# Cross attention's query and output products: from split weights to plain fp32, one token half after the other

## What is computed

```python
x = x + merged @ w_out                             # "wo2": the mixer's output product
h = rmsnorm(x, norm_xa_g)
q = (h @ w_q).reshape(B, S, 4, 128)                # "xq"
k, v = split(rmsnorm(mem, norm_mem_g) @ w_kv)      # made earlier in the kernel
p = softmax(einsum("bshd,bmhd->bhsm", q, k) * 128 ** -0.5)
x = x + einsum("bhsm,bmhd->bshd", p, v) @ w_o      # "xo"
h = rmsnorm(x, norm_ffn_g)
qq = (h @ w_q_peer).reshape(T, 8, 2, 128)          # "pq": the expert queries
s = einsum("thpd,hpnd->thpn", qq, subkeys)         # head scores, two lists of 128 a head
# top 16 of each list, top 16 of their 256 sums: 16 experts e with softmax weights g
a = gelu(einsum("td,thkd->thk", h, w_down[e]))
x = x + einsum("thk,thkd->td", g * a, w_up[e])
return rmsnorm(x, final_g)
```

## Time and profile before

| | us |
|---|---|
| median of 3 runs | 1304.25 |
| lowest and highest | 1302.63, 1304.44 |
| profiled execution, its span | 1302.2 |
| PE busy | 1188.0 (91%) |
| DVE busy | 920.6 (71%) |
| ACT busy | 545.5 (42%) |
| POOL busy | 285.0 (22%) |
| bytes moved by the DMA engines | 396.67 MB, of them 268.45 MB by gathers |

### The profile page before, as it was taken

The page is one execution under the profiler, slowest core; times in us unless marked ns, Lnnn a source line. Parts: engine busy times, 40 slices in busy tenths (PEclk is TensorE's granted clock), DMA queues, the critical chain, the costliest instruction groups (busy, mean ns, idle before and its releaser), DMA issues.

```text
span 1302.2 us, 16734 instructions
## 1 busy us (share of the span) xinstructions
PE 1188.0 (91%) x5950; PEld 845.7 (65%) x5950; DVE 920.6 (71%) x1836; ACT 545.5 (42%) x983; POOL 285.0 (22%) x261
## 2 busy tenths in 40 slices
PE   9999999999999999999999889999777877777776
PEld 9998999888888999998865545545322332332322
DVE  6885858777854865567797777776767777777655
ACT  5833655566533547536643333322322222222312
POOL 0000000000000000000145455443643444544420
PEclk9999999999999999999999999999999999989999
DMA  7544456455655654456799999999999999999996
GB/s 287 194 166 148 167 200 213 169 178 183 225 195 194 213 176 160 164 196 230 318 408 402 420 419 420 419 420 419 420 420 418 421 419 422 419 422 419 420 420 262
DMA packets 55925, 396.67 MB, mean 305 GB/s; under 512 B 6320, under 2 KB 6320, under 8 KB 8624
## 3 DMA queue, kind: packets, MB, share of 16 engines
q0 software_dynamic: 36864, 268.45, 49.9%
q1 hardware_dynamic: 17136, 119.16, 25.6%
q10 hardware_dynamic: 1856, 8.13, 1.8%
HBM read 394.67 MB, written 1.05 MB: 304 GB/s over the span
## 4 chain that ended last, share of the span: by engine, by line
PE 56%; DMA 31%; DVE 6%; issue 3%; ACT 3%; POOL 2%; DVEq 0%; POOLq 0%; ACTq 0%
DMA R<-experts,IDX 31%; PE ps L606 19%; PE ps L707 10%; PE ps L1190 8%; PE ps L926 4%; PE ps L654 3%; PE ps L928 2%; POOL R L2778 2%; PE ps L618 2%; DVE R L2564 2%; PE ps L674 1%; PE ps L1041 1%; PE ps L1095 1%; ACT DIAG L1645 1%; PE ps L1068 1%
## 5 line engine op out<-in xcount | busy, mean ns | idle before, releaser
L1190 PE MATMUL ps<-R,DIAG 128*128 128x512 f32 x1020 | 484.6, 623 | 102.7 <-ACT DIAG L1645 97.5
L1190 PEld LDWEIGHTS ps<-R,DIAG 128*128 128x128 f32 x1020 | 191.5, 197 | 371.3 <-issue 206.9
L2564 DVE CUSTOM_DVE_ANT_0 R<-R,XN 128x1024 f32<-128x1024 f32 x256 | 313.4, 1227 | 143.5 <-DMA R<-experts,IDX 137.8
L2778 POOL DMA_INDIRECT R<-experts,IDX x256 | 283.7, 1108 | 535.4 <-PE ps L1190 278.4
L1774 DVE TENSOR_TENSOR w_lo<-raw,w_hi 128x1024 fp32r<-128x1024 f32 x204 | 241.7, 1220 | 89.3 <-ACT w_hi L1243 84.9
L1243 ACT ACTIVATE w_hi<-raw 128x1024 fp32r<-128x1024 f32 x203 | 204.7, 1051 | 78.0 <-DMA raw<-weights 78.0
L1633 ACT ACTIVATE act_d<-dots,rst 128x2 f32<-128x2 f32 (+1 forms) x130 | 38.5, 296 | 329.4 <-DVE dots L2564 329.2
L1645 ACT ACTIVATE DIAG<-con,coef 128x128 f32<-128x128 f32 x255 | 88.6, 394 | 121.3 <-DVE coef L2573 118.1
L606 PE MATMUL ps<-both_C,w_hi 128*128 128x256 f32 x576 | 105.3, 284 | 0.3 <-ACT GA L1277 0.3
L2758 POOL TENSOR_SCALAR_AFFINE_SELECT WS<-WS 128x1024 f32<-128x1024 f32 x1 | 1.1, 1085 | 439.0 <-DMA BS<-gbs 439.0
L606 PEld LDWEIGHTS ps<-both_C,w_hi 128*128 128x128 f32 x576 | 90.3, 192 | 1.4 <-issue 0.8
(11 more groups left out here) (407 smaller groups left out, 1734.2 us busy)
## 6 DMA issues: line engine op xcount, KB each, us to landing
raw<-weights SPq DMA_DIRECT2D x103, 1024.0 KB, 4.8
PQW<-weights SPq DMA_DIRECT2D x6, 1024.0 KB, 9.4
R<-experts,IDX POOLq DMA_INDIRECT x256, 31.8
LNR<-rows ACTq DMA_DIRECT2D x3, 1024.0 KB, 4.7
raw<-weights SPq DMA_DIRECT2D x4, 512.0 KB, 8.4
XF<-xT SPq DMA_DIRECT2D x2, 512.0 KB, 5.6
MEM<-mem ACTq DMA_DIRECT2D x1, 1024.0 KB, 5.0
XR<-x ACTq DMA_DIRECT2D x1, 1024.0 KB, 7.8
```

Source lines behind the costliest of these rows:

```text
L1190: mm = pe.matmul(psum[:, 4 + 2 * m + n, :], DIAG[:, k, :], rows_[:, D + n * 512:D + (n + 1) * 512], start=(it % 8 == 0 and k == 0), stop=True,
L2564: dve.tensor_tensor_reduce(out=rows_[:, 0:D], in0=rows_[:, 0:D], in1=XN[:, m, :], scale=1.0, scalar=0.0, op0=ALU.mult, op1=ALU.add, accum_ ...
L2778: pool.indirect_dma_start(out=R[u][:, :], out_offset=None, in_=experts, in_offset=bass.IndirectOffsetOnAxis(ap=IDX[:, it, k:k + 1], axis=0 ...
```

## The change

- `xq` and `xo` are computed in plain fp32 on the blocks as loaded (`XQ`, `XO`). These four blocks are not split, nor are their other operands.
- `cross_query` is turned round: the weights stand still and the tokens stream, 32 products of 128 columns a half, so the query comes out already turned. `query_turn`, `cross_rows` and `cross_across` with their copies go. The gain is a column of `vec` and is multiplied in behind the turn of `XR` (`rows_gained`, `second_side`). The norm's factor goes into the softmax's scale, and so off the query's path.
- The output product, `cross_out`, is 8 products of 512 columns a half; for the first half the last 512 columns are done in two parts, so that turning and the first expert query start in between.
- Of `wo2`, blocks 0 and 1 are loaded and split early, in buffers of their own (`early_raw`, `early_hi`, `early_lo`). PE does all of the first half's `wo2` before the second half's, whose rows are spread over the first half's cross attention (`second(n)`).
- The second half's query product and scores now stand behind the first head scores.
- The buffers of the expert query weights, of `H3`, `H4` and others move, and with them `OPENED`: what each of the first eight gathers waits for. The gains `LNR` are loaded once, not twice.

The core of the diff (declarations, ACT's and DVE's orders ahead of the first head scores, and what only renames are left out):

```diff
-        OPENED = {0: (11, None), 1: (18, None), 2: (8, VALUES_END)}
-        FIRST_XO_END = half_end(BLOCK["xo"])
-        s0 = BLOCK["xo"] % 4
-        for n, u in enumerate((s0, 4 + s0)):
-            OPENED[3 + n] = (u, FIRST_XO_END)
-        for n, u in enumerate((s0 + 1, 5 + s0, 12)):
-            OPENED[5 + n] = (u, XO_END)
...
+        OPENED = {0: (18, ("xo_a", 3)), 1: (11, ("xo_a", 3)), 2: (12, ("xo_a", 3)), 3: (1, ("xq_b", 1)),
+                  4: (2, ("xq_b", 1)), 5: (8, ("values", 1)), 6: (5, ("xo_b", 2)), 7: (6, ("xo_b", 2))}
...
+            ma, gm, wo2, xq, xo = (BLOCK[n] for n in ("ma", "gm", "wo2", "xq", "xo"))
+            load(ma + 1, slot_of(ma + 1), half_end(ma - 3))
+            whole(early_raw[0], wo2, early_in[0])
+            load(gm, slot_of(gm), half_end(ma - 2))
+            sp.wait_ge(gm_ready, 2)
+            whole(early_raw[1], wo2 + 1, early_in[1])
+            load(gm + 1, slot_of(gm + 1), half_end(ma - 1))
+            load(wo2 + 2, slot_of(wo2 + 2), half_end(ma))
+            load(wo2 + 3, slot_of(wo2 + 3), half_end(ma + 1))
+            for n in range(2):
+                sp.wait_ge(gemm_done, half_end(gm + n))
+                whole(XQ[n], xq + n, xq_in[n])
             sp.wait_ge(m2_ready, 4)
-            load_query(2)
-            load_query(3)
-            for j in range(2):
-                load(BLOCK["xo"] + j, (BLOCK["xo"] + j) % 4, half_end(BLOCK["wo2"] + 2 + j))
-            load_query(6)
-            load_query(7)
-            for j in range(2):
-                load(PQ0 + j, (PQ0 + j) % 4, half_end(BLOCK["xq"] + j))
-                load_query(4 + j)
+            for j in range(3):
+                whole(PQW[j], PQ0 + j, pq_in[j])
...
+                whole(XO[n], xo + n, xo_in[n])
+            sp.wait_ge(gemm_done, half_end(wo2 + 3))
+            for j in range(3, 8):
+                whole(PQW[j], PQ0 + j, pq_in[j])
...
+            def cross_query(m, half):
 
                 r = RING["xq"] + m
-                for k, h in pieces:
-                    b = BLOCK["xq"] + k
-                    if (k, h) == (0, 0):
-                        free_bank(r)
-                    w = take(b % 4, half_end(b, h))
-                    has_lo(pe, *norm_parts(m, k))
-                    for i in (2 * h, 2 * h + 1):
-                        for n, (a, o) in enumerate(parts(w, opB)):
-                            mm = pe.matmul(bank(r), o[:, 4 * k + i, m * P:(m + 1) * P],
-                                           a[:, 2 * i:2 * i + 2, :].rearrange("p a b -> p (a b)"),
-                                           start=(k == 0 and i == 0 and n == 0),
-                                           stop=(k == 1 and i == 3 and n == 2), skip_group_check=True)
-                    if m:
-                        mm.then_inc(gemm_done, 1)
-                    elif (k, h) == (1, 1):
-                        mm.then_inc(half_done, 1)
-
-            def query_turn(m):
+                if half == 0:
+                    free_bank(r)
+                pe.wait_ge(xq_in[half], 16)
+                wait_aux(pe, *(("h3Ta", half) if m == 0 else (("h3Tb", "h3Tc")[half], 0)))
+                for h in range(XH):
+                    for k in range(4):
+                        mm = pe.matmul(bank(r)[:, h * P:(h + 1) * P],
+                                       XQ[half][:, 2 * k + h // 2, (h % 2) * P:(h % 2 + 1) * P],
+                                       H3[m][:, 4 * half + k, :], start=(half == 0 and h == 0 and k == 0),
+                                       stop=(half == 1 and k == 3), skip_group_check=True)
+                if half:
+                    mm.then_inc((xq_a, xq_b)[m], 1)
...
-            both_sides("wo2", opC, "m2")
-            side_half("wo2", opC, 1, 0, 0, 0)
-            side_half("wo2", opC, 1, 0, 0, 1)
-            turn_side("h3Ta", 0, 0, 0, 1)
-            side_half("wo2", opC, 1, 0, 1, 0)
-            side_half("wo2", opC, 1, 0, 1, 1)
-            cross_query(0, [(0, 0), (0, 1)])
-            turn_side("h3Ta", 1, 0, 1, 2)
-            side_half("wo2", opC, 1, 1, 0, 0)
-            cross_query(0, [(1, 0), (1, 1)])
-            side_half("wo2", opC, 1, 1, 0, 1)
-            turn_side("h3Tb", 0, 1, 0, 3)
-            query_turn(0)
-            side_half("wo2", opC, 1, 1, 1, 0)
+            def cross_out(m, g, cols=slice(0, 512), bank_=None):
+
+                bank_ = 4 + 2 * m + g if bank_ is None else bank_
+                pe.wait_ge(xo_in[g], 16)
+                for i in range(4):
+                    mm = pe.matmul(psum[:, bank_, cols], AX_[m][:, i, :],
+                                   XO[g][:, 2 * i:2 * i + 2, :].rearrange("p a b -> p (a b)")[:, cols],
+                                   start=(i == 0), stop=(i == 3), skip_group_check=True)
+                mm.then_inc((xo_a, xo_b)[m], 1)
+
+            for i in range(8):
+                wo2_rows(0, 0, i)
+            for i in range(4):
+                wo2_rows(1, 0, i)
+            turn("h3Ta", 0, "wo2", 1, XR, 0, range(4))
+            for i in range(4, 8):
+                wo2_rows(1, 0, i)
+            second(1)
+            turn("h3Ta", 1, "wo2", 2, XR, 0, range(4, 8))
+            cross_query(0, 0)
+            cross_query(0, 1)
+            second(1)
             cross_scores(0, 0)
             cross_scores(0, 1)
-            side_half("wo2", opC, 1, 1, 1, 1)
-            cross_query(1, [(0, 0)])
+            second(6)
             cross_turn(0, 0)
+            second(2)
             cross_turn(0, 1)
-            cross_query(1, [(0, 1)])
-            turn_side("h3Tc", 0, 1, 1, 4)
+            second(4)
             cross_values(0)
-            cross_query(1, [(1, 0), (1, 1)])
-            has_lo(pe, *values_parts(0))
-            side("xo", AXo, 0, 0)
-            side("xo", AXo, 1, 0)
-            query_turn(1)
-            turn_side("h4Ta", 0, 0, 0, 5)
+            turn("h3Tb", 0, "wo2", 3, XR, 1, range(4))
+            second(2)
+            wait_aux(pe, "xpva")
+            cross_out(0, 0)
+            cross_out(0, 1, slice(0, 256))
+            turn("h4Ta", 0, "xo", 1, XR, 0, range(4))
+            wait_wide(pe, "wo2", 3)
+            cross_out(0, 1, slice(256, 512), 6)
+            turn("h4Ta", 1, "xo", 2, XR, 0, range(4, 6))
+            free_bank(RING["pq"])
+            free_bank(RING["xq"] + 1)
+            pe.wait_ge(pq_in[0], 16)
+            wait_aux(pe, "h4Ta", 0)
+            query_part(0, 0, 0, range(4))
+            turn("h4Ta", 2, "xo", 3, XR, 0, range(6, 8))
+            query_part(0, 0, 1, range(4))
+            for j in (1, 2):
+                wait_aux(pe, "h4Ta", j)
+                for c in range(2):
+                    mm = query_part(0, 0, c, (2 * j + 2, 2 * j + 3))
+                    if j == 2:
+                        mm.then_inc(query_a if c else first_half, 1)
+            turn("h3Tc", 0, "wo2", 4, XR, 1, range(4, 8))
+            head_scores(0, 0)
+            cross_query(1, 0)
+            cross_query(1, 1)
             cross_scores(1, 0)
             cross_scores(1, 1)
-            turn_side("h4Ta", 1, 0, 1, 6)
-            query(0, 0)
+            query(1, 0)
             cross_turn(1, 0)
-            head_scores(0, 0)
             cross_turn(1, 1)
-            query(1, 0, (0,))
             cross_values(1)
-            query(1, 0, (1,))
             head_scores(1, 0)
-            has_lo(pe, *values_parts(1))
-            side("xo", AXo, 0, 1)
-            side("xo", AXo, 1, 1)
-            query(2, 0)
+            query(2, 0, (0,))
+            wait_aux(pe, "xpvb")
+            cross_out(1, 0)
+            cross_out(1, 1)
+            query(2, 0, (1,))
             query(3, 0, (0,))
             head_scores(2, 0)
...
+            act.wait_ge(first_half, 1)
+            act.activation(QP[:, 0, 0:P], bank(RING["pq"])[:, 0:P], ACT.Copy).then_inc(first_query, 1)
+            act.wait_ge(query_a, 1)
+            drain(act.activation(QP[:, 1, 0:P], bank(RING["pq"] + 1)[:, P:T], ACT.Copy), "pq", 0)
+            second_side(1)
+            warm(ACT.Exp)
+            cross_across_second()
+            cross_exps(1, 0)
+            cross_exps(1, 1)
+            gate_exp(0)
+            queries(1, 0)
             cross_turned(1, 0)
             cross_turned(1, 1)
-            warm(ACT.Sqrt)
-            root_side(3, 0)
-            values_hi(1)
-            queries(1, 0)
+            warm(ACT.Gelu_apprx_tanh)
             head_scores(1, 0)
-            gate_exp(0)
-            warm(ACT.Gelu_apprx_tanh)
+            values(1)
             gelu(0, 0)
+            diagonals(0, 0)
             queries(2, 0)
-            diagonals(0, 0)
+            activate(0, 1)
             head_scores(2, 0)
-            square_side("xo", 3, 1, 0)
-            activate(0, 1)
...
-            values_lo(1)
             inverse_side(3, 0)
+            dve.wait_ge(rows2_in, 16)
+            gain_side(0, first_cols)
+            gain_side(0, last_cols)
             second_eight()
+            cross_max(1, 0)
```

(17 more changed lines are left out.)

499 lines of the change are left out of this document (241 added, 258 removed).

## The result

The changed kernel takes 1315.11 us (median of 5, 1314.08 to 1315.54) against 1304.25 (1302.63 to 1304.44): a ratio of 1.0088, 95% interval 1.0078 to 1.0099, so 10.9 us or 0.8% slower. The forecast was 1311.0, slower, in a range up to 1316.5. The profiled execution has a span of 1313.8 us, 11.6 more than the 1302.2 of the earlier trace rows.

What follows compares the result with a forecast made beforehand. DMA row gathers at 2.50 us each bound the end, throttled from gather 8 by PE's sums. H 7.0 us earlier, S 8.1 later; end 5.6 to 8.1 later, 6.8 taken: span 1309.0 plus 2.05, 1311.0 us; range 1302.5 to 1316.5.

Steps and rivals of the forecast that it cites:

- H: Time when the first head scores are read; forecast 633.5 us, 7.0 earlier, bounds 632.7 to 634.7.
- S: Time when the weighted sums begin on PE; forecast 666.9 us, 8.1 later, bounds 664.6 to 669.6.
- The prices on PE: Plain fp32 products per half: query 7.2 us against 5.4 split, output 6.9 against 5.44.
- The early splits at nothing: Three blocks split before 585.7, costed at nothing though 6.3 us more on ScalarE and 7.3 on VectorE.
- VectorE's chain from H: From H through candidates, gains, second half's maxima, exponentials and gate to the two weightings: 17.1 us.
- PE behind it, 16.3 us: PE's path from the weightings to S: turn, copy, values, head scores, expert queries, second output product; 16.3 us.
- The resumption of the stream at gather 8: Gather 8 waits for two rows, flow from 672.8; 248 gathers at 2.50 us end 5.6 us later.
- gather 19: Row gather issued at 690.94 before; with PE's order from S on unchanged, it comes 7 to 8 us later.
- Lead kept: Rival: the end follows gather 0, issued 7.0 us earlier, giving 1297.3 us; chance 0.12.
- Cancel: Rival: H at its low bound, short waits, S near 662, no change, 1302 to 1306 us; chance 0.14.
- More is lost: Rival: VectorE stalls behind ScalarE's order, or PE's clock falls; 3 to 6 us on top, 1314 to 1317; chance 0.12.
- Dips in the stream: Gather stream after S: dips like 361 GB/s at 684 to 692 can return; their absence marks a failed step.

Runs made afterwards that it cites:

- no lead: The changed kernel with its first three gathers made to wait for the second half's query product: 1314.87 us.
- other blocks: The changed kernel with the second output product reading the weight blocks of expert queries 6 and 7, so two opening buffers are free early: 1316.14 us.
- Kept busy: The changed kernel with 28 matmuls of the third expert query also run once for nothing in PE's wait before the turn: 1312.51 us.
- buffers swapped: The changed kernel with the buffers of gathers 0 and 1 swapped, so gather 8 needs one row of sums instead of two: 1315.06 us.
- filled wait: The changed kernel with the whole third expert query in PE's wait before the turn and half the fourth before the second output product: 1309.60 us.
- sums sooner: The filled wait with the fourth query and third head scores moved among the sums and VectorE's gains behind the second half's maxima: 1310.08 us.
- output between: As sums sooner, with the first pair of sums between the two column halves of the second output product: 1314.11 us.
- output twice: The changed kernel with the second half's output product computed twice: 1321.82 us.

## Why the prediction was right, and where its sum was too small

*Direction and mechanism.* Right: the first gather moved ahead (H at 634.29, within 632.7 to 634.7), the sums moved back (S at 670.75, 1.15 beyond the upper bound of 669.6), and the end went with the sums. The size was too small: 6.8 us said, 10.9 measured. The time lies inside the stated range because that had been widened for the rivals; it is just outside the forecast's own, 1307.5 to 1315. That the early start is worth nothing is shown by no lead and by other blocks.

*The prices on PE.* Right. The query product of the first half took 7.16 us (7.2 said), the output product 6.87 by the distance of its neighbours (6.9 said). The work up to H was 47.5 us with 0.4 of waits where I had 46.7 and 1.1; the sum came out right with both parts off.

*The early splits at nothing.* Right: PE is busy 23.70 of 23.70 us up to the mixer product, and VectorE 19.34, less full than the 21.2 I feared. The product began at 586.4 instead of 585.7, which is most of the 0.8 us by which H was late; PE met no wait there, so I put that to the time ahead of it and can't say more.

*VectorE's chain from H.* Right: its second weighting ends at 651.59, 17.3 us after H (17.1 said). PE's wait before the turn is 3.07 us where the sum gives 3.7 (17.1 less 13.4): the turn starts behind the first weighting, not the second. The other wait, 0.85 us, is the 0.9 that the sum has as a copy.

*PE behind it, 16.3 us: the step that failed.* It took 19.2 (651.59 to 670.75). I priced the turn, the values and the scores at full clock, and named a fall of the clock only to wave it off, with a wait of 1.78 us that had none and a page of forty slices with one low slice. One shorter wait is no evidence for a longer one, and a slice of 33 us can't show 6.8 us. Kept busy shows its size: 2.6 us of time. It is the larger part of what was missing; a term for it, which I priced at "as much" as 3 to 6 us in a rival, belonged in the forecast's sum.

*The resumption of the stream at gather 8: one term too small, and not the only place.* I put gather 8 at S + 2 x 1.73 + 0.2, which is S + 3.7. The rows said more: before, it came 2.76 us behind S with one row to wait for (658.83 to 661.59), so with two it is near 4.5; measured are 4.4. I counted 248 gathers from there and got 5.6 us, took 8.1 (all of S's shift) as the upper bound, and chose 6.8. With the measured gather 8 the count gives 1312.3, 1.5 below the span. But gather 19 gives as late an end, and buffers swapped and other blocks show that an earlier gather 8, 5 or 6 alone brings nothing. I had named gather 19, with the unchanged order of PE from S on, and used it for a bound only. It would have given 8.1, and with the measured S 11.9; the profile has 11.8 for gather 19 and 11.6 for the end. So of the 4.8 us missing in the span 0.8 are H, 3.1 the way from H to S (2.9 of it PE's part, most of that the clock), and about 1 this step.

*The rivals.* "Lead kept" is refuted by no lead. "Cancel" would have needed S near 662; the filled wait shows that 664.4 was in reach with another order, not with this one. "More is lost", which had 0.12, holds the measured time (1314 to 1317). Its main mechanism is wrong: VectorE does stand idle for 4.98 us, but from S to gather 19 takes 32.0 us as against 32.1, so nothing was lost there. Its other one, the fall of the clock, is what happened. *Dips in the stream* did not come back: before there were 361 GB/s at 684 to 692, and in the changed kernel, once gather 8 flows, no window of 4 us up to 724 is under 406. That was one of my signs that a step fails.

*Still open:* a version that beats the kernel before measurably. By the sum above the filled wait is bound by gather 6, at 664.4, and that by the work between H and the second output product's end; sums sooner and output between show that moving work behind S moved the loss and did not remove it.

## What to carry to other kernels

When a stream is throttled by an engine that frees its buffers, make the sum for every transfer that waits for the engine (its issue, plus the stream's time for it and all behind it) and price the change by the latest, not by the first transfer nor by the one at which the stream starts again. Where a later one gives as late an end, filling a hole early only digs one later, as two kernels here show. Before you price work behind a new wait of a few microseconds, ask what it would cost if TensorE's clock fell there, and look for work that has to be done anyway to put into the wait; here that was worth 5.5 us, half of it for the wait and half for the clock.

## What the hardware showed that I had not expected

PE's wait of 3.01 to 3.08 us came with the lower clock in all five kernels that had it (changed, no lead, output twice, buffers swapped, other blocks). Shorter waits went either way: those of 1.78 us before and 2.51 in sums sooner kept a clock of 1.00, and that of 2.31 did in the changed kernel and six others, but in other blocks the same 2.31 were followed by half clock from 690, and in the filled wait one of 1.87 us by half clock from 704. The low stretch was not of one length either: 6.8 us in the changed kernel, some 3.5 in no lead and in other blocks, at the same work. And useless matmuls made a kernel faster by 2.6 us.
